# Two-layer decoder trunk on one core: weights held in two buffers, one pipeline from layer 0's output to the shared keys, plain fp32 attention in layer 1

## What is computed

```python
u = rms_norm(h, a_norm_g) * (1 + scale) + shift            # layer 0
q, k, v, z = split(u @ a_w_in, 4)                           # q, k normed per 64 columns
o = diff_causal_attention(q, k, v, lam, slopes)             # 8 heads of 2 sub-heads, causal
o = rms_norm(o, a_subln_g) * 0.8 * silu(z)
h = h + gate * (o @ a_w_out)
ukv = rms_norm(h, kv_norm_g) * (1 + kv_scale) + kv_shift    # shared keys and values
k_s, v_s = split(ukv @ w_kv, 2)                             # 2 heads of 64; k_s normed
u = rms_norm(h, b_norm_g) * (1 + scale) + shift             # layer 1
q, z = split(u @ b_w_in, 2)                                 # q normed per 64 columns
o = sliding_window_sink_attention(q, k_s, v_s, sinks)       # 16 heads, window 128
h = h + gate * ((o * silu(z)) @ b_w_out)
```

## Time and profile before

| | us |
|---|---|
| median of 3 runs | 1358.45 |
| the profiled execution | 1358.09 |
| its span, first to last instruction | 1356.3 |
| PE busy | 1174.1 (87%) |
| DVE / ACT / POOL busy | 856.5 / 700.0 / 232.9 |

### The profile page before, as it was taken

The page is one execution under the profiler, slowest core; times in us unless marked ns, Lnnn a source line. Parts: engine busy times, 40 slices in busy tenths (PEclk is TensorE's granted clock), DMA queues, the critical chain, the costliest instruction groups (busy, mean ns, idle before and its releaser), DMA issues.

```text
span 1356.3 us, 22457 instructions
## 1 busy us (share of the span) xinstructions
PE 1174.1 (87%) x6192; PEld 928.2 (68%) x6192; DVE 856.5 (63%) x2676; ACT 700.0 (52%) x2161; POOL 232.9 (17%) x354
## 2 busy tenths in 40 slices
PE   0469899998989899998975997679999898985998
PEld 0457576676757676675754885568888787875886
DVE  6665766666676766667664324976887888776221
ACT  0655555555555556555554104966776776674100
POOL 1201212112121211212101221111211212110122
PEclk9989999999999999999997998879999999997999
DMA  8342131312222131222214334110020100113332
GB/s 296 118 139 65 50 101 42 111 55 87 71 72 85 57 101 42 89 71 69 86 39 144 122 126 171 63 63 5 13 75 17 58 31 24 62 32 112 116 122 85
DMA packets 53226, 111.42 MB, mean 82 GB/s; under 512 B 5904, under 2 KB 19216, under 8 KB 52112
## 3 DMA queue, kind: packets, MB, share of 16 engines
q1 hardware_dynamic: 53136, 110.51, 24.8%
HBM read 93.71 MB, written 16.78 MB: 81 GB/s over the span
## 4 chain that ended last, share of the span: by engine, by line
PE 69%; DVE 12%; issue 8%; ACT 6%; DMA 3%; POOL 1%; DVEq 1%; POOLq 0%; ACTq 0%; SPq 0%
PE ps_p L591 12%; PE ps_p L593 11%; PE ps_p L592 11%; PE ps_s L671 5%; PE ps_o L706 3%; PE ps_t L731 3%; PE ps_p L815 2%; PE ps_p L816 2%; PE ps_p L817 2%; PE ps_o L817 2%; PE ps_o L815 2%; PE ps_o L816 2%; PE ps_t L792 2%; ACT e L952 2%; PE ps_s L744 2%
## 5 line engine op out<-in xcount | busy, mean ns | idle before, releaser
L591 PE MATMUL ps_p<-w_hi,u_hi 128*128 128x512 f32 x768 | 332.8, 433 | 13.0 <-DVE w_lo L1165 12.5
L593 PE MATMUL ps_p<-w_hi,u_lo 128*128 128x512 f32 x768 | 303.9, 396 | 0.0
L592 PE MATMUL ps_p<-w_lo,u_hi 128*128 128x512 f32 x768 | 302.8, 394 | 0.0
L591 PEld LDWEIGHTS ps_p<-w_hi,u_hi 128*128 128x128 f32 x768 | 146.2, 190 | 73.5 <-ACT ez L983 23.7
L593 PEld LDWEIGHTS ps_p<-w_hi,u_lo 128*128 128x128 f32 x768 | 145.4, 189 | 33.4
L592 PEld LDWEIGHTS ps_p<-w_lo,u_hi 128*128 128x128 f32 x768 | 146.9, 191 | 18.3
L952 ACT ACTIVATE e<-e,negm 128x256 f32<-128x256 f32 (+7 forms) x128 | 98.3, 769 | 113.4 <-DVE negm L1301 112.7
L1323 DVE TENSOR_REDUCE ssum<-sq 128x4 f32<-128x256 f32 x64 | 26.8, 419 | 122.2 <-ACT sq L978 122.2
L1018 ACT ACTIVATE pT<-ps_t 128x512 f32<-128x512 f32 (+2 forms) x96 | 44.6, 490 | 103.8 <-PE ps_t L731 103.3
L671 PE MATMUL ps_s<-kTa,qTa 64*128 64x512 f32 (+3 forms) x384 | 89.1, 541 | 8.3 <-DVE negm L1301 5.3
L1125 ACT ACTIVATE kT<-ps_t 128x512 fp32r<-128x512 f32 x32 | 17.4, 595 | 152.8 <-PE ps_t L828 152.8
(11 more groups left out here) (185 smaller groups left out, 2603.5 us busy)
## 6 DMA issues: line engine op xcount, KB each, us to landing
adabuf<-ada_w SPq DMA_DIRECT2D x64, 384.0 KB, 3.2
raw<-w_a SPq DMA_DIRECT2D x80, 256.0 KB, 3.4
raw<-w_b SPq DMA_DIRECT2D x48, 256.0 KB, 3.2
e<-ada_w SPq DMA_DIRECT2D x4, 1024.0 KB, 4.8
stage<-ada_w SPq DMA_DIRECT2D x4, 1024.0 KB, 4.9
e<-x SPq DMA_DIRECT2D x8, 512.0 KB, 3.4
oa_scratch<-ob SPq DMA_DIRECT2D x64, 64.0 KB, 1.6
e<-oa_scratch SPq DMA_DIRECT2D x8, 512.0 KB, 4.7
```

The costliest lines, as they stand in the source:

```text
L591: pe.matmul(o, u_hi[:, c, t], w_hi[:, c, :], start=(c == 0), stop=False)
L592: pe.matmul(o, u_hi[:, c, t], w_lo[:, c, :], start=False, stop=False)
L593: mm = pe.matmul(o, u_lo[:, c, t], w_hi[:, c, :], start=False, stop=(c == KD - 1))
```

## The change

- `w_hi` and `w_lo` become lists of two buffers, taken in turn by unit. The units are walked in pairs (`unit_pairs`), so that the buffer's number is a constant. In slot i of unit u chunk i-1 of unit u+1 is split (ACT, then DVE; POOL splits only unit 0's), the last chunk in slot 0 of its own unit. `w_free` is gone. `raw` is a ring of 4 chunks.
- The output weights go to `w_hi[0]`, `w_hi[1]` (halves 0 and 1), and `u_hi`, `u_lo` are free for the next layer. The gain of o (`C_SUB`) moves from these weights to `oT`, which holds one tile, split by halves.
- `output(0, 0, True)` is one pipeline over tiles: output of tile s-1, norm of h1 of tile s-2 straight from `adabuf`, keys and values of tile s-3 (8 plain fp32 products of 256 columns), key norm and transposes of tile s-4, and after the last tile the first two projections of layer 1. `norm(NT, True)`, the reload of h1 and the splits for the keys are gone. The weights of layer 1's first unit are split after slot 8.
- `attn_b` has the form of `attn_a` (depth 5): scores as one fp32 product of 64 rows and 256 columns per head, p not split, two fp32 products of 64 columns per head with `va`, no split of q.

New code that sets the order (lines left out are marked):

```diff
+            def load_chunk(unit, c, src):
+                at_least(sp, w_lo_done, 8 * unit + c - RAW + 1)
+                sp.dma_start(raw[:, c % RAW, :], src).then_inc(w_loaded[c], 16)
+            def attn_io(S, units, w_src, unit0, width, o_dram, is_a):
+                def slot(u, i, par, live):
...
+                    if live(0):
+                        load_chunk(u + unit0 + 1, i, w_src[u + 1, :, i, :])
+                    if not live(0) and i < 4:
+                        for c in (2 * i, 2 * i + 1):
+                            load_chunk(units + 1 + unit0, c, w_src[units + 1, :, c, :])
+                    if not live(0) and i == 4:
+                        sp.wait_ge(S.pt, units * (UNIT_CHUNKS if is_a else NT))
...
+            def out_io(S, units, res_src, o_dram, dst, n0, with_next):
+                for s in range(NT + 1):
+                    n1 = s - 1
+                    if s < NT:
+                        m = n0 + s
+                        if s >= 2:
+                            sp.wait_ge(c_tr, 2 * (m - 1))
...
+                            sp.dma_start(e0[:, s % 2, :], o_dram[s * P:(s + 1) * P, :]).then_inc(c_o[s % 2], 16)
...
+                        at_least(sp, c_sum, m)
...
+                        sp.dma_start(flat(stage[:, 0:2, :]), res_src[s * P:(s + 1) * P, :]).then_inc(c_res, 16)
+                        if s == 0 and with_next:
+                            sp.dma_start(wkv, w_kv).then_inc(wkv_loaded, 16)
+                    if s == NT and with_next:
+                        for c in range(RAW, KD):
+                            load_chunk(U_B, c, w_b[0, :, c, :])
+                    if n1 >= 0:
+                        sp.wait_ge(c_sum, n0 + n1 + 1)
+                        sp.dma_start(dst[n1 * P:(n1 + 1) * P, :],
+                                     adabuf[:, (n1 % 2) * D:(n1 % 2 + 1) * D]).then_inc(c_st[n1 % 2], 16)
+                    if with_next and s in (2, 3, 4, 5):
+                        load_chunk(U_B, s - 2, w_b[0, :, s - 2, :])
...
@@ PE @@
+                for s in range(NT + (4 if with_next else 1)):
+                    n1, n2, n3, n4 = s - 1, s - 2, s - 3, s - 4
+                    if 0 <= n1 < NT:
+                        half(n1, 0)
+                    if s < NT:
+                        pe.wait_ge(c_o[s % 2], 16 * (m // 2 + 1))
+                        at_least(pe, c_lo, 2 * m)
...  (8 transposes of e0 into ps_t)
+                    if with_next and 0 <= n3 < NT:
...  (8 products into ps_o[:, n3 % 2, 0:256], stage and wkv)
+                    if with_next and 0 <= n2 < NT:
+                        pe.wait_ge(m_norm, n2 + 1)
...  (8 transposes of the normed h1 into ps_s)
+                    if with_next and 0 <= n4 < NT:
...  (2 transposes of qn)
+                    if 0 <= n1 < NT:
+                        half(n1, 1)
+                    if with_next and s in (NT + 1, NT + 2):
+                        project(b, False, 0, 0, s - NT - 1, s - NT - 1, range(KD))
@@ ACT, in a slot of attention, behind the copies to qT and ahead of those to pT @@
+            def split_for(S, u, i, par, live, units, unit0):
+                if not live(0):
...
+                elif i:
+                    split_hi(u + unit0 + 1, i - 1, 1 - par)
+                elif not (isinstance(u, int) and u == 0):
+                    split_hi(u + unit0, KD - 1, par)
@@ ACT, output @@
...  (norm, modulations and u_hi of tile s-2)
+                    if s < NT:
+                        m = n0 + s
+                        for g in range(2):
+                            act.wait_ge(c_tr, 2 * m + g + 1)
+                            if s:
+                                act.wait_ge(*((c_free, m) if g == 0 else (c_mm, 2 * m)))
...  (oT[:, 0, half g])
+                    if with_next and s == NT:
+                        act.wait_ge(c_mm, 2 * NT - 1)
+                        for c in range(KD):
+                            split_hi(U_B, c, 0)
@@ DVE, output @@
+                    if with_next and 0 <= n2 < NT:
+                        product(n2, 1)
...  (the norm's chain of tile s-2, key norm of s-4)
+                    if 0 <= n1 < NT:
+                        product(n1, 0)
+                        if not with_next:
+                            product(n1, 1)
...  (modulations, u_lo of tile s-2)
+                    if s < NT:
...  (oT[:, 1, half g] for g in 0, 1)
+                    if with_next and s == NT:
+                        for c in range(KD):
+                            split_lo(U_B, c, 0)
@@ PE, layer 1's attention @@
-                    pe.matmul(o, p_hi[:, t], vs[:, i5 - 1 + k, :], start=(k == first), stop=False)
-                    mm = pe.matmul(o, p_lo[:, t], vs[:, i5 - 1 + k, :], start=False, stop=(k == 1))
+                    mm = pe.matmul(ps_o[:, i4 % 2, j * HD:(j + 1) * HD], pT[:, (2 * j + k) * P:(2 * j + k + 1) * P],
+                                   va[:, i4 - 1 + k, (j // 2) * HD:(j // 2 + 1) * HD], start=(k == k0), stop=(k == 1))
```

More of the change, by code:

```diff
@@ L47 @@
 ADAW = 768
+RAW = 4
 C_VEC = 0
@@ L80, in stand_alone, with unit_pairs, flat, groups @@
     eng.sem_inc(passed, 1)
[L83 to L104, removed]
+def unit_pairs(eng, units, lags, slot):
+    for i in range(16):
+        slot(i // 8, i % 8, i // 8, lambda lag, i=i: i >= lag)
+    with eng.Fori(1, units // 2) as blk:
+        for i in range(16):
+            slot(2 * blk + i // 8, i % 8, i // 8, lambda lag: True)
+    for i in range(lags):
+        slot(units, i, 0, lambda lag, i=i: i < lag)
+def flat(t):
+    return t.rearrange("p a n -> p (a n)")
+def groups(t, c):
+    return t.rearrange("p (g c) -> p g c", c=c)
+def build(nc, x, par, rows_in, ada0_w, ada1_w, w_a, w_kv, w_b, out):
     h1 = nc.dram_tensor("h1_scratch", [SEQ, D], F32).ap()
@@ L119, in build @@
         u_lo = sb("u_lo", [P, KD, SEQ], F32R)
[L120 to L137, removed]
+        w_hi = [sb(f"w_hi{k}", [P, KD, FW], F32R) for k in range(2)]
+        w_lo = [sb(f"w_lo{k}", [P, KD, FW], F32R) for k in range(2)]
+        oT = sb("oT", [P, 2, D], F32R)
+        raw = sb("raw", [P, RAW, FW])
+        kT = sb("kT", [P, 2, SEQ])
+        qT = sb("qT", [P, 2, 256])
+        va = sb("va", [P, NT, P])
+        pT = sb("pT", [P, 1024])
         e0 = sb("e0", [P, 2, 1024])
@@ L317, in build, with w_ready @@
-        V_KV, V_B = A_HEADS, A_HEADS + 1
+        def w_ready(eng, unit, c):
+            eng.wait_ge(w_lo_done, 8 * unit + c + 1)
         @block.sync
         def _(sp):
[L322 to L352, removed]
@@ L401, in slot @@
-                    if isinstance(blk, int) and blk == 0 and i == 1:
-                        early()
-                    if not live(0) and i == 0:
-                        late()
-                pipeline(sp, 2, NT // 2, 2, slot)
-            sp.wait_ge(ada0_used, KD)
-            norm_loads(x, 0, False)
-            sp.wait_ge(ada0_mm, 1)
-            attn_io(a, A_HEADS, w_a, 0, 0, P, o_a, True)
-            def kv_weights():
-                for c in range(KD):
-                    sp.wait_ge(w_lo_done, 8 * (U_OUT_A + 1) + c + 1)
-                    sp.dma_start(raw[:, c, 0:256], w_kv[:, c, :]).then_inc(w_loaded[c], 16)
@@ L561, in _, with project @@
         def _(pe):
-            def adaln_first():
-                pe.wait_ge(s_const, 4)
-                pe.wait_ge(ada0_used, KD)
-                for j in range(ADA0 // P):
-                    mm = pe.matmul(ps_p[:, 0, j:j + 1], adabuf[:, j * P:(j + 1) * P], ones[:, :], start=True, stop=True)
-                mm.then_inc(ada0_mm, 1)
-            def project(S, is_a, u, it, n, chunks):
+            def project(S, is_a, u, par, it, n, chunks):
                 o = ps_p[:, it % 2, :]
-                if not len(chunks):
-                    return
+                first = isinstance(u, int) and u == 0
```

1330 lines of the change are left out of this document (560 added, 770 removed).

## The result

The changed kernel takes 1368.1 us (median of 6 runs, 1363.5 to 1375.5) against 1358.0 for the kernel before: ratio 1.008, 95% interval 1.0052 to 1.0108. It is slower by 0.8%, where 1317 us was forecast. The profiled execution took 1370.4 us, its span is 1368.6 us (before 1356.3), at a mean granted clock of 0.953 (before 0.967).

What follows compares the result with a forecast made beforehand. PE's work was taken to bound the full stretches, chains over ACT, DVE, POOL and SP the others. Terms -35 + 1 - 7 + 12 - 13 - 18 + 19 = -41 gave span 1315, forecast 1317 us, range 1284 to 1343.

Steps and rivals of the forecast that it cites:

- start, to the first scores: Start: chunk loads between x's loads wait for POOL's splits, x tiles 2 and 3 about a microsecond later; +1 us (0 to +2).
- layer 0's attention, 7 handovers: Layer 0: next unit's weights ready, so 4.1 to 4.8 us of each handover slot's 15.0 go; -35 us (-27 to -37).
- first drain: Drain after layer 0's attention: o loaded earlier, first product near 727 instead of 734.4; -7 us (-4 to -9).
- layer 0's output to layer 1's projections: Stage of 187.3 us before: load stalls, half clock, tail and cold start make it 199; +12 us (+1 to +21 by the keys).
- layer 1's attention: Layer 1: slot work hardly changes, 3 handovers of about 5 us go, less a microsecond; -13 us (-8 to -36).
- second drain: Drain after layer 1's attention, 41.0 us before: one slot fewer of depth and shorter chains; -18 us (-10 to -21).
- output of layer 1: Last stage, 96.0 us before: PE waits 1.5 us for DVE and 1.4 for the load of o per slot; +19 us (+9 to +26).
- R1: Both output stages: loads of o cost their issue only, no stall or half clock; 1276 us, chance 10%.
- R3: Both attention stages: the split in every slot falls on the chain, 1.2 us per slot, +106; 1423 us, chance 5%.
- R4: Layer 0: new unit still waits for its last chunks, half the handover gains stay away, +24; 1341 us, chance 8%.
- SP's list: First output stage: load of o queued behind the store, landing after 4.4 us; PE stalls 3.8 us in six slots.
- R2: Layer 1's output: short waits pull the clock down as in the norm stage, +20; 1337 us, chance 15%.

Runs made afterwards that it cites:

- experiment 7: Changed kernel with the weight splits inside the looped units of both attention stages cut from 512 columns to one: 1366.0 us.
- experiment 1: Changed kernel with SP issuing the load of o one turn earlier, ahead of the wait for POOL's sum, in both output stages: 1294.7 us.
- Experiment 2: Changed kernel with the load of o for tile s+1 still behind the wait for POOL's sum, but ahead of the other transfers: 1316.3 us.
- experiment 3: Changed kernel with added PE products, results overwritten, ahead of the wait for the load of o (22 in first output stage, 10 in last): 1354.3 us.
- Experiment 8: Changed kernel with early load of o, earlier oT copies, chunk loads spread at the start, layer 1's first split cut in two, its first projection moved: 1266.4 us.
- experiment 6: Changed kernel with the loads of o for tiles 2 to 7 of both outputs issued from ACT's list one turn earlier: 1297.7 us.

## Why the prediction was wrong

Term by term, in us of the span (forecast; measured as the difference of the stages before and after, on the same cuts, the last to the end of the span):

| term | forecast | measured |
|---|---|---|
| start, to the first scores | +1 | +5.1 |
| layer 0's attention, 7 handovers | -35 | -32.0 |
| first drain | -7 | -7.7 |
| layer 0's output to layer 1's projections | +12 | +26.5 |
| layer 1's attention | -13 | -2.5 |
| second drain | -18 | -17.4 |
| output of layer 1 | +19 | +40.3 |
| sum | -41 | +12.3 |

**Right.** The handovers of layer 0 (15.0 to 10.6 us in the slot of the earlier trace rows, forecast 10.2 to 10.4), the cover of the splits (experiment 7), both drains (in the first the data of o came 3 us earlier than counted, but the end of DVE's last splits set the start, as forecast), the cost of the keys (3.4 us per tile forecast, 3.45 at full clock), of the eight fp32 products with values (1.7 us), and the tail behind tile 7 (39 us with the cold start forecast, 37.6 to the scores measured, from 877.2 to 914.8). Rivals R1, R3 and R4 didn't come. R1's mechanism is what experiment 1 builds by hand.

**The load of o, landing (step "SP's list").** The mechanism was named, its size taken too small. The forecast took 4.4 us to land from the earlier trace rows, a stage in which only the store goes out ahead of the load, 0.6 to 1.0 us before it. In the new order the sum releases the residual's load, the store, a chunk of weights and the load of o in one burst. In the first output stage the load leaves 4.1 to 4.6 us after DVE's product starts (counted: 3.9) and lands after 5.8 to 6.6 us, and the wait is 5.0 to 6.2 us instead of 3.8 (34.6 in sum, forecast 22.8). In the last it lands after 5.3 to 6.1 us, and the wait is 2.7 to 3.1 instead of 1.4 (16.7, forecast 8.4). That is 20 of the 53 us of error (from -41 to +12.3). Experiment 2 shows the burst's part: loads at the head of it land in 4.3 and 4.1 us.

**The clock in layer 1's output (step "output of layer 1", rival R2).** Priced at nothing in the forecast, at 20 us in R2. Behind five of the six waits for the load PE runs at half rate for a time; the granted clock there is 0.50, the lower level of 1.2 GHz (windows of the changed kernel: 1268.05 to 1270.6 right behind a wait of 2.66 us):

```profile
1268.05:1270.60 2.55, 2.55 (x10) 2.43 (x11) 0.00 (x0) 0.00 (x0) 0.00 (x0) 0.50 0.03 6
```

With the waits removed 11 us more than the waits themselves came back (experiment 2: 27.0 less 16). In the first output stage the clock was in the sum with 6 x 1.7 = 10.2. The slow transposes and keys behind the six waits add up to 12.5, of which experiments 2 and 3 give back 10.5 and 10.9. So R2's mechanism is there, at half its price.

**Layer 1's attention.** What the forecast took off the second drain as "one slot fewer of depth" was partly moved, not removed. The lines view of PE for the two stages, of before (921.7 to 1213.1), then of after (913.6 to 1202.5), each for scores, products with values and transposes:

```profile
L744 PE MATMUL ps_s<-kT,qT 128*128 128x256 f32 (+1 forms) x233 | 32.4, 281 | 1.2 <-PE ps_p L593 1.2
L773 PE MATMUL ps_o<-vs,p_hi 128*128 128x256 f32 x208 | 51.3, 284 | 4.2 <-issue 4.2
L792 PE MATMUL ps_t<-ident,e 128*128 128x128 f32 x216 | 28.4, 273 | 1.2 <-ACT qT L1084 1.2
```

```profile
L565 PE MATMUL ps_s<-kT,qT 64*128 64x256 f32 (+1 forms) x248 | 34.0, 394 | 0.5 <-ACT qT L800 0.5
L581 PE MATMUL ps_o<-va,pT 128*128 128x64 f32 x432 | 51.3, 271 | 0.0
L597 PE MATMUL ps_t<-ident,e 128*128 128x128 f32 x224 | 29.3, 272 | 0.0
```

Beside 30 projections there are now the scores of 31 tiles instead of 29 (8 instructions a tile), the products with values of 27 instead of 26 (16 instructions a tile; before 8 for the high part, and 8 more for the low one on another line), the transposes of 28 instead of 27: 2 x 1.06 + 1.70 + 0.79 = 4.6 us that stood in the drain before. The first projection behind the cold start adds 1.8 (its first 12 products take 4.6 us, 2.8 at full clock). Six products of that projection, 1.4 us, stand ahead of the cut in the kernel before and behind it here. The handovers did go, but gave 11.2 us and not 13: the second and third are worth 4.6 each (a unit takes 76.7 us instead of 81.3, of which PE waits 0.65 for DVE's `gbuf` at the unit's end), the first only 2.0. That is 9.6 of the 10.5 us that are missing; 1 us stays open.

**Start.** Forecast +1, measured +5.1 (95.50 to 100.58 us at the first scores). SP's timeline of the changed kernel shows tile 3's load of x behind two chunk loads whose wait ended only at 53.0 us:

```profile
47.43 0.33 SPq L356 DMA_DIRECT2D e<-x  x1
53.00 1.55 SPq L291 DMA_DIRECT2D raw<-w_a  x2
54.59 4.10 SPq L356 DMA_DIRECT2D e<-x  x2
```

Experiment 8 gives 1.6 to 3.5 us of it back, by the kernels it is compared with. The rest stays open.

**Layer 0.** 3 us of the missing gain are at the loop's edge (last section).

In sum the 53 us are: longer waits for the load 20, clock behind them 13 (11 in the last output, 2 in the first), layer 1's attention 10.5, start and layer 0 7, and some 2 spread over joints and the tail. The sign turned on the waits for one load. The change pays 64 us against before once that load is early, and the range was too narrow because it held no case in which waits that were foreseen were half as long again in six slots and twice as long in six more.

One bound of the working is off without bearing on this: with the keys at 2.3 us instead of 3.4 in eight tiles the stage of the first output comes to +3, not +1.

## What to carry to other kernels

A load that stands behind a wait in an issuer's list costs that wait, its place in the burst that the wait releases, and the clock behind it. So look at each in-order list for the first consumer in time, and issue its load as soon as its buffer is free. Remove waits in the order in which they end: the same edit was worth 0 us with a later wait behind it and some 10 us without. And when a pipeline gets shallower, count which work of the drain turns up in the stage ahead.

## What the runs showed of the hardware

**Issue in a burst.** As the fourth DMA in a row the load of o takes 1.20 us to issue (791.54 above), the three ahead of it 0.33 to 0.43. The fourth place alone doesn't make it: in experiment 2 the chunk of weights stands there, half as large, and takes 0.43 (SP's queue):

```profile
776.63 0.43 SPq L291 DMA_DIRECT2D raw<-w_b  x1
```

The same 512 KB land in 3.3 us from ACT's list, which issues them between SP's bursts (experiment 6), in 4.1 to 4.3 (medians) at the head of SP's burst, in 4.4 behind the store alone, in 5.3 to 6.1 as the third and in 5.8 to 6.6 as the fourth.

**Waits of equal length, different clock.** In the changed kernel's last output the eight transposes ran at half rate (1.97 us) behind a wait of 2.66 us and at full rate (1.10 us) behind one of 2.75; in experiment 2's first output at half behind 2.77 us, at full behind 3.48 (PE's timelines, first of the changed kernel, then of experiment 2):

```profile
1268.05 1.97 PE L628 MATMUL ps_t<-ident,e 128*128 128x128 f32 x8 [2.66 <-DMA e<-ob_scratch]
1286.07 1.10 PE L628 MATMUL ps_t<-ident,e 128*128 128x128 f32 x8 [2.75 <-DMA e<-ob_scratch]
...
721.67 1.09 PE L628 MATMUL ps_t<-ident,e 128*128 128x128 f32 x8 [3.48 <-DMA e<-oa_scratch]
758.14 1.97 PE L628 MATMUL ps_t<-ident,e 128*128 128x128 f32 x8 [2.77 <-DMA e<-oa_scratch]
```

The length of the wait alone doesn't tell what the clock does. All six waits of 5.0 to 6.2 us in the changed kernel's first output stage were followed by half rate. What else it hangs on was not tried.

**The edge of a loop.** At both edges between iterations of the loop over layer 0's units ACT waits for nothing that the profile shows, and PE for DVE behind it (ACT's and PE's timelines of the changed kernel):

```profile
361.68 0.39 ACT L709 ACTIVATE sq<-ps_p 128x256 f32<-128x256 f32 x1 [2.44 <-issue]
...
364.39 0.70 PE L481 MATMUL ps_s<-kT,qT 64*128 64x256 f32 x4 [1.84 <-DVE negm L993]
```

The slot takes 12.8 and 12.5 us there instead of 10.9. The wait of 2.0 to 2.4 us is in every one of the nine kernels with this change, and not in ACT's timeline of that stage in the kernel before. What it is stays open: no run was made on it.
